# Routing of a mixture-of-experts layer: pair-summed variance, choice of experts in two token halves, block owners on partitions

## The reference

```python
x = layer_norm(DEEPNORM_ALPHA * x + y, ln1_g, ln1_b)
g_logits = x @ w_rg + b_rg                       # 4 groups
grp = argmax(g_logits); p_grp = softmax(g_logits)[grp]
e_logits = (x @ w_re + b_re)[grp]                # 8 experts of that group, 32 in all
top_val, top_idx = top_k(e_logits, 2)
gate = softmax(top_val) * p_grp
# tokens sorted by expert, padded to blocks of rows; every block has one expert
ys = silu(rows @ w_gate[e]) * (rows @ w_up[e]) @ w_down[e], times gate, summed per token
```

## Time and profile before

| | us |
|---|---|
| median of 3 runs | 3631.74 (3631.66 to 3636.03) |
| the profiled execution: its own time | 3633.96 |
| its span, first to last instruction | 3632.7 |
| PE busy in the span | 3414.1 (94%) |
| DVE, ACT, POOL busy | 1570.4, 900.4, 261.7 |

### The profile page before, as it was taken

How to read it: one execution, slowest core, us unless ns; L and a number is a source line. 1 busy time by engine, 2 the same in 40 slices (tenths; PEclk the granted TensorE clock), 3 DMA queues, 4 the chain that set the end, 5 groups by cost and what they waited for, 6 DMA issues and landing times.

```text
span 3632.7 us, 30841 instructions
## 1 busy us (share of the span) xinstructions
PE 3414.1 (94%) x12338; PEld 1862.6 (51%) x12338; DVE 1570.4 (43%) x2766; ACT 900.4 (25%) x1750; POOL 261.7 (7%) x251
## 2 busy tenths in 40 slices
PE   9999998899989899999999999998889997999997
PEld 3468546666654344444444565673447444444443
DVE  6355476466631555444634112324656233211114
ACT  4110453377741100000000111223334031111112
POOL 0012232000000000000000000000000002222221
PEclk9999999999999999999999999999999997999999
DMA  5024212000022111111211101002000108999994
GB/s 229 35 75 167 83 63 90 22 1 1 1 81 93 58 47 47 36 45 36 94 35 41 64 24 41 19 26 82 1 14 11 48 24 340 372 368 369 366 367 164
DMA packets 63243, 370.58 MB, mean 102 GB/s; under 512 B 6826, under 2 KB 13242, under 8 KB 37500
## 3 DMA queue, kind: packets, MB, share of 16 engines
q1 hardware_dynamic: 40492, 187.71, 14.2%
q0 software_dynamic: 22608, 180.89, 13.2%
HBM read 329.16 MB, written 39.41 MB: 101 GB/s over the span
## 4 chain that ended last, share of the span: by engine, by line
PE 83%; DVE 8%; ACT 7%; issue 1%; DMA 1%; SPq 0%; another core or an unknown queue 0%; POOL 0%; DVEq 0%; ACTq 0%; POOLq 0%
PE ps L1298 14%; PE ps L2533 9%; PE ps L1421 7%; PE ps L1596 6%; PE ps L2552 4%; PE ps L837 3%; PE ps L2190 3%; PE ps L1237 3%; PE ps L1598 3%; PE ps L984 2%; PE ps L703 2%; PE ps L840 2%; PE ps L1012 2%; PE ps L646 2%; ACT arena L1064 2%; PE ps L2030 1%
## 5 line engine op out<-in xcount | busy, mean ns | idle before, releaser
L1298 PE MATMUL ps<-arena 128*128 128x512 f32 x1232 | 532.1, 594 | 9.5 <-DVE arena L1324 9.5
L1298 PEld LDWEIGHTS ps<-arena 128*128 128x128 f32 x1232 | 234.3, 190 | 307.0 <-issue 287.1
L2533 PE MATMUL ps<-arena 128*128 128x512 f32 x752 | 331.7, 594 | 0.0
L1421 PE MATMUL ps<-arena 128*128 128x512 f32 x616 | 264.6, 592 | 0.0
L2491 POOL DMA_INDIRECT arena<-in_wgu_dram,arena x47 | 44.1, 939 | 2666.5 <-DVE arena L2450 2414.0
L2533 PEld LDWEIGHTS ps<-arena 128*128 128x128 f32 x752 | 139.8, 191 | 158.1 <-issue 158.1
L1596 PE MATMUL ps<-arena 128*128 128x512 f32 x480 | 209.0, 596 | 0.0
L1421 PEld LDWEIGHTS ps<-arena 128*128 128x128 f32 x616 | 116.6, 189 | 147.9 <-issue 143.8
L1119 DVE TENSOR_SCALAR_CACHE_REDUCE arena<-ps 128x1280 f32<-128x1280 f32 x96 | 139.3, 1488 | 110.1 <-PE ps L984 110.1
L837 PE MATMUL ps<-arena 128*128 128x512 f32 (+1 forms) x432 | 174.7, 558 | 0.0
L2552 PE MATMUL ps<-arena 128*128 128x512 f32 x376 | 169.1, 592 | 0.5 <-DVE arena L2603 0.5
(11 more groups left out here) (375 smaller groups left out, 4943.4 us busy)
## 6 DMA issues: line engine op xcount, KB each, us to landing
arena<-in_wmod_dram SPq DMA_DIRECT2D x24, 1024.0 KB, 5.5
yslot<-arena SPq DMA_DIRECT2D x47, 512.0 KB, 8.7
arena<-in_wup_dram SPq DMA_DIRECT2D x22, 1024.0 KB, 4.8
arena<-in_wout_dram SPq DMA_DIRECT2D x16, 1024.0 KB, 4.8
arena<-in_cf_dram SPq DMA_DIRECT2D x12, 1024.0 KB, 4.8
arena<-in_wdn_dram SPq DMA_DIRECT2D x16, 704.0 KB, 4.0
arena<-in_w2b_dram SPq DMA_DIRECT2D x9, 1024.0 KB, 4.8
arena<-in_ci_dram SPq DMA_DIRECT2D x16, 512.0 KB, 3.5
```

The lines of the kernel that those rows point to most:

```text
L1298: ins = mm(bk(b), left[:, k], right[:, k], k == 0, k == 3)
L1421: ins = mm(bk(b), sb(left + k * 128, 128), right(k), k == 0, k == 10)
L2533: ins = mm(bk(b), sb(XB + i % 2 * 1024 + k * 128, 128), sb(WGU[i % 3] + k * 512, 512), k == 0, k == 7)
```

## The change

- Variance of half 1: ScalarE squares the 8 tiles into 8 buffers, VectorE adds them in pairs, and PE sums the 4 pair sums in bank 7, after the logits of half 0. Half 0 is as before.
- `act_lnscale` raises its event for each tile; the logits wait for each tile.
- `pe_route` has a ring of six banks, and the order: logits 0, pair variance, turning of logits 0, tokens 0 to 3, logits 1, turning of logits 1, tokens 4 to 7, ranks, owners, slots.
- `dve_choose` runs once per half; the gates are formed behind the sums of the choices.
- `dve_place`: block b's owner is found on partition b alone, put on a diagonal and spread over the partitions by a matmul with ones; `widx` comes between the two choices' one-hot work.

```diff
-        for k in range(8):
-            yield from pe_variance(1, k)
+    def pe_pair_variance():
+        yield from claim(7)
+        for k in range(4):
+            P.wait_ge(*(yield ("lnpair", k)))
+            ins = mm(bk(7), con("o1024"), sb(SQ2 + 2 * k * 512, 512), k == 0, k == 3)
+        ins.then_inc(*P.step(("lnv", 1, 7)))
+        held[7] = [("lnx", 1)]
...
+        if tc:
+            A.wait_ge(*(yield ("lnv", 0, 7)))
+        elif k > 3:
+            A.wait_ge(*(yield ("lnv", 0, k - 4)))
...
-        yield from dve_lnscale(1)
+        for k in range(4):
+            V.wait_ge(*(yield ("lnsq", 1, 2 * k + 1)))
+            a, b = (sb(SQ2 + (2 * k + i) * 512, 512) for i in range(2))
+            vt.tensor_tensor(a, a, b, ADD).then_inc(*V.step(("lnpair", k)))
...
+    def pe_logits(tc, banks):
+        n, b = nth["wrt"][0], next(banks)
+        yield from claim(b)
+        P.wait_ge(*wready(n))
+        for k in range(8):
+            P.wait_ge(*(yield ("ln", tc, k)))
+            ins = mm(bk(b, 512, 0, 36), sb(wat(n) + k * 36, 36), sb(XT + k * 1024 + tc * 512, 512), k == 0, k == 7)
...
+        held[b] = [("lt", tc)]
...
+    def pe_turn_logits(tc, banks):
...
+        held[b] = [("lg", tc)]
+
+    def pe_route():
+        banks = ring(range(6))
+        yield from pe_logits(0, banks)
+        yield from pe_pair_variance()
+        yield from pe_turn_logits(0, banks)
+        for j in range(4):
+            yield from pe_tokens(j, banks)
+        yield from pe_logits(1, banks)
+        yield from pe_turn_logits(1, banks)
         for j in range(4, 8):
             yield from pe_tokens(j, banks)
...
+        P.wait_ge(*(yield ("bdiag",)))
+        mm(bk(b, NBLK), con("ones", 0, NBLK), bdiag[0:NBLK], True, True).then_inc(*P.step(("owners",)))
...
     def act_route():
+        for tc in range(2):
+            js = range(4 * tc, 4 * tc + 4)
+            if tc == 0:
+                for j in js[:2]:
+                    yield from act_tokens(j)
+            A.wait_ge(*(yield ("gex", tc)))
+            st.activation(half(ge, tc), half(ge, tc), ACT.Exp).then_inc(*A.step(("gee", tc)))
+            if tc == 0:
+                for j in js[2:]:
+                    yield from act_tokens(j)
+            A.wait_ge(*(yield ("edx", tc)))
+            st.activation(half(ed, tc), half(ed, tc), ACT.Exp).then_inc(*A.step(("ede", tc)))
         for j in range(4, 8):
             yield from act_tokens(j)
...
     def dve_choose():
+        yield from dve_logits(0)
+        yield from dve_lnscale(1)
+        yield from dve_choose_half(0)
+        yield from dve_logits(1)
+        yield from dve_choose_half(1)
...
-        vt.tensor_tensor(cv, incl.rearrange("p (u e) -> p u e", u=1).broadcast_to([128, NBLK, 32]),
-                         con("bidx").rearrange("p (b u) -> p b u", u=1).broadcast_to([128, NBLK, 32]), ALU.is_le).then_inc(*V.step())
...
+        vt.tensor_scalar(owner, incl, con("pidx"), None, ALU.is_le).then_inc(*V.step())
+        vdone()
+        vt.tensor_reduce(bcol, owner, AX.X, ADD).then_inc(*V.step())
+        vdone()
+        vt.tensor_scalar(bcol, bcol, 31.0, 128.0, ALU.min, MUL).then_inc(*V.step())
+        vdone()
+        vt.tensor_scalar(bdiag, con("ident")[:, 0:NBLK], bcol, None, MUL).then_inc(*V.step(("bdiag",)))
         for q, oh in enumerate((oh1, oh2)):
             x, d, du, fb, pm = dest[q]
+            if q:
+                V.wait_ge(*(yield ("owners",)))
+                vt.tensor_scalar(be, bk(bank["owners"], NBLK), con("pidx"), None, ADD).then_inc(*V.step())
+                vdone()
+                vt.tensor_copy(widx.bitcast(U32), be).then_inc(*V.step(("widx",)))
+            vdone()
```

More of the change, by code:

```diff
@@ L2199, in pe_wout2 @@
             yield from pe_mean(tc, 7)
-        for k in range(8):
-            yield from pe_variance(1, k)
+    def pe_pair_variance():
[5 more added lines that the diff above has]
+        held[7] = [("lnx", 1)]
     def act_lnsq(tc, k):
         A.wait_ge(*(yield ("cent", tc, k)))
-        if tc or k > 3:
-            A.wait_ge(*(yield ("lnv", tc - (k < 4), (k - 4) % 8)))
-        st.activation(sb(SQ2 + k % 4 * 512, 512), sb(XT + k * 1024 + tc * 512, 512), ACT.Square).then_inc(*A.step(("lnsq", tc, k)))
+        if tc:
+            A.wait_ge(*(yield ("lnv", 0, 7)))
+        elif k > 3:
+            A.wait_ge(*(yield ("lnv", 0, k - 4)))
+        st.activation(sb(SQ2 + (k if tc else k % 4) * 512, 512), sb(XT + k * 1024 + tc * 512, 512), ACT.Square).then_inc(*A.step(("lnsq", tc, k)))
     def act_lnscale(tc):
@@ L2214, in act_lnscale @@
             A.wait_ge(*(yield ("lnh", tc, k)))
-            st.activation(xx, xx, ACT.Identity, bias=par("l1b", k)).then_inc(*A.step(("ln", tc)))
+            st.activation(xx, xx, ACT.Identity, bias=par("l1b", k)).then_inc(*A.step(("ln", tc, k)))
     def act_wout2():
@@ L2308, in sp_tokens @@
             dma.dma_start(out=x_d[j * 128:(j + 1) * 128, :], in_=sb(XK + j * 1024, 1024)).then_inc(*LD.turn(("xd", j)))
-    def pe_route():
-        banks = ring(range(8))
-        n = nth["wrt"][0]
+    def pe_logits(tc, banks):
+        n, b = nth["wrt"][0], next(banks)
+        yield from claim(b)
         P.wait_ge(*wready(n))
[L2314 to L2325, removed]
+        for k in range(8):
+            P.wait_ge(*(yield ("ln", tc, k)))
+            ins = mm(bk(b, 512, 0, 36), sb(wat(n) + k * 36, 36), sb(XT + k * 1024 + tc * 512, 512), k == 0, k == 7)
+        bank[("logit", tc)] = b
+        ins.then_inc(*P.step(("logit", tc)))
+        held[b] = [("lt", tc)]
+    def pe_turn_logits(tc, banks):
         b = next(banks)
         yield from claim(b)
[L2328 to L2333, removed]
+        P.wait_ge(*(yield ("lt", tc)))
+        for j in range(4):
+            ins = turn(bk(b, 36, off=36 * j), sb(LT + tc * 512 + j * 128, 128, 0, 36), con("ident", 0, 36)[:, 0:36])
+        bank[("lgt", tc)] = b
+        ins.then_inc(*P.step(("lgt", tc)))
+        held[b] = [("lg", tc)]
[4 more added lines that the diff above has]
+        yield from pe_turn_logits(0, banks)
+        for j in range(4):
+            yield from pe_tokens(j, banks)
+        yield from pe_logits(1, banks)
+        yield from pe_turn_logits(1, banks)
         for j in range(4, 8):
@@ L2344, in pe_route @@
         yield from claim(b)
+        P.wait_ge(*(yield ("bdiag",)))
+        mm(bk(b, NBLK), con("ones", 0, NBLK), bdiag[0:NBLK], True, True).then_inc(*P.step(("owners",)))
+        bank["owners"] = b
+        held[b] = [("widx",)]
+        b = next(banks)
+        yield from claim(b)
         for q in range(2):
@@ L2353, in act_route, with half @@
     def act_route():
[L2354 to L2359, removed]
+        for tc in range(2):
[10 more added lines that the diff above has]
+            st.activation(half(ed, tc), half(ed, tc), ACT.Exp).then_inc(*A.step(("ede", tc)))
         for j in range(4, 8):
             yield from act_tokens(j)
+    def half(a, tc):
+        return a[:, 4 * tc:4 * tc + 4]
     def dve_pick(v, ri, n, one, tmp):
@@ L2367, in dve_pick @@
         vdone()
-        vt.tensor_tensor(e, v, m.broadcast_to([128, 8, n]), ALU.is_equal).then_inc(*V.step())
+        vt.tensor_tensor(e, v, m.broadcast_to([128, 4, n]), ALU.is_equal).then_inc(*V.step())
         vdone()
-        vt.tensor_tensor(e, e, wide(ri, n), MUL).then_inc(*V.step())
+        vt.tensor_tensor(e, e, con(ri).rearrange("p (u e) -> p u e", u=1).broadcast_to([128, 4, n]), MUL).then_inc(*V.step())
         vdone()
@@ L2373, in dve_pick @@
         vdone()
-        vt.tensor_tensor(one, e, m2.broadcast_to([128, 8, n]), ALU.is_equal).then_inc(*V.step())
+        vt.tensor_tensor(one, e, m2.broadcast_to([128, 4, n]), ALU.is_equal).then_inc(*V.step())
     def groupwise(a):
-        return a.rearrange("p j (g u) -> p (j g) u", u=1).broadcast_to([128, 32, 8])
+        return a.rearrange("p j (g u) -> p (j g) u", u=1).broadcast_to([128, 16, 8])
     def dve_round(a):
@@ L2384, in dve_round @@
         vdone()
-    def dve_choose():
[L2387 to L2424, removed]
```

52 lines of the change are left out of this document (44 added, 8 removed).

## The result

The changed kernel takes 3626.39 us (median of 11 runs, 3624.44 to 3632.64), the kernel before 3633.6 (11 runs, 3631.66 to 3640.24). The ratio is 0.9979, with a 95% interval of 0.9970 to 0.9987: 0.21% faster, between 0.13% and 0.30%. The profiled execution has a span of 3625.0 us, where it was 3632.7.

A forecast was written before the change was run, and what follows sets the result against it. PE bounds the 47 expert blocks, which follow their start, so the chain of waits in the 77 us before counts. 0.8 + 3.7 + 2.7 - 1.2 = 6.0 us off 3631.74 gives 3625.7; range 3621.0 to 3630.5.

The forecast's parts named there:

- likeliest case: Whole kernel: a change within 0.2% (7.3 us), which a measurement can't tell from none; chance 0.63.
- Variance: Half 1's variance: PE's sums end at 2968.4 instead of 2972.94; root and scaling shift by 4.5 us.
- Logits 1: Half 1's logits: banks hold PE idle 8.4 us, the clock drops, they end at 2991.4 against 2992.23; 0.8 us gained.
- T: The moment logits 1 end, put at 2991.4; 2992.3 if transposes don't count as busy for the clock.
- half-wide steps: Half 1's choice of experts, from logits 1 to the rank matmuls: 13.67 us less 4.8 leaves 8.9.
- Token 7: Its transposes wait for ScalarE's copies of token 4, so ranks start 10.0 us behind logits 1; net 3.7 us gained.
- Place: Block owners and slots: shorter owner steps, widx between the choices; 2.7 us gained (bounds 2.4 to 3.0).
- Gathers: Token gathers land later, behind block 0's weights and the gain tables; 1.2 us lost (ends 0 and 2).
- Logits of 36 columns: Rival: logits 1 don't bring the clock back and take 13.8 us instead of 9.0; 3630.5 us, chance 0.09.
- DMA doesn't bound the experts: Denies the rival that DMA bounds the expert stage and everything follows widx: gain 3.2 us, 3628.5, chance 0.06.
- gathers did not share with the weights behind them: Denies the slower rival: gathers served along with weights of blocks 1 and 2, block 1 turned at 3042; 3641, chance 0.04.
- kept clock: Rival: PE's clock is not lost or returns soon, gathers hardly late; gain 9 us, 3622.5, chance 0.13.

The follow-up runs named there:

- e6: Changed kernel with half 1's 8 squares summed by TensorE one by one, without VectorE's pair sums; ratio to the kernel before 0.9988.
- e1: Changed kernel with logits 1 put before tokens 2 and 3 on TensorE; ratio to the kernel before 0.9973.
- e3: Changed kernel with nine unread 512-column matmuls added in TensorE's idle time before token 2's second transposes; ratio to the kernel before 0.9968.
- e4: Changed kernel with ScalarE's copies of tokens 4 and 5 before the second exponential of half 1; ratio to the kernel before 0.998.
- b1: Kernel before with the block owners' part of the change alone; ratio to the kernel before 0.9991.
- e7: Changed kernel with widx made before the first choice's one-hot work instead of between the two; ratio to the kernel before 0.9978.
- e2: Changed kernel with SyncE's two 0.5 MB gain tables loaded after the second block's output; ratio to the kernel before 0.9981.
- b2: Kernel before with the pair sums of half 1's squares alone, in the variance's old place; ratio to the kernel before 0.9994.

## Why the prediction was right, point by point

The median was put at 3625.7 and came out at 3626.39, while the kernel before, timed beside it, had 3633.6 instead of 3631.74: a gain of 7.2 where 6.0 was forecast, 6.5 of it in the trace. The likeliest case was within 0.2%; measured is 0.21%, with an interval on both sides of that bound.

Term by term, to the first expert matmul, the forecast was 0.8 + 3.7 + 2.7 - 1.2 = 6.0, and the traces give 0.91 + 3.78 + 2.96 - 1.48 = 6.17. The first two terms hold in mechanism and size. That the sum fits so well is partly luck: the last two are off by 0.26 and 0.28 in opposite directions.

- **Variance.** Forecast to end at 2968.4, 10.4 behind the means; 10.62. (Logits 0 were put to 2964.9, where 2958.0 and 7.06 are 2965.06; in the trace their last comes 6.99 behind the means.) That step and the shift of 4.5 us in the scaling (4.3: 2974.74 less 2958.57, against 20.46 before) held. e6 shows the pairs are worth 3.45 of it.
- **Logits 1.** The bank count decided this, and held: PE idle 8.4 us forecast, 8.51 seen, ended by the named bias add; half clock; T gained 0.8 forecast, 0.91 seen. e1 and e3 show both halves of the reason, the queue's order and the clock. Two details were off and cancelled: logits 1 began 0.4 us later than put (the bias add came later, and the 12 transposes took 2.99 us without a pause, not 2.8 with pauses for the copies), and they took 8.54 us instead of 9.0, because the clock returned 2.9 us into them and not 3.9.
- **The half-wide steps.** 13.67 less 4.8 us was to leave 8.9; in e4, where nothing else holds the ranks, they start 8.75 behind logits 1 (42.03 less 33.28).
- **Token 7.** Forecast at T + 10.0, seen at T + 9.90, with ScalarE's copy as the releaser. e4 gives 1.17 back. "By then likely at half clock" was right by little, which is luck: the clock fell just as these transposes began. In e3, where it stayed up, the ranks start 9.14 behind logits 1.
- **Place.** From the ranks' start to the token gather's issue 20.44 before, 17.48 after: 2.96 against 2.7. Some 0.25 of it is the ranks themselves (1.93 instead of 2.18 us to VectorE's first step), because they follow the transposes without a pause and the clock returned under the last of them. Without that, in b1, it is 2.68 (20.44 less 17.76).
- **Gathers.** 1.2 lost forecast, 1.48 measured (8.22 to 9.70). The sign held, and its cause, the shorter lead of the weights, is shown for the first gather by e7. The size is luck in part. Bytes alone, from 3023.0 on, would have both gathers in by 3025.7, as early as the shift alone; the 1.2 us from there to 3026.9 stand on no row. e2 took out a quarter of the bytes for 0.4 us, e7 gave the old lead back and recovered 0.81 of the 1.48, and b2, with the old lead, stands at 9.10 where the kernel before has 8.22. `widx` came 7.22 us behind the ranks' end (7.4 forecast), and the weights were issued 3.78 sooner (3.2 forecast).
- **Rivals.** Logits of 36 columns did bring the clock back (2986 to 2987), so that one falls (the slot matmuls, its argument, did leave the clock at 0.50 here too, 3011 to 3019). DMA doesn't bound the experts: the weights are issued 3.78 us sooner, the last gather 6.48. The gathers did not share with the weights behind them to the point of a loss: the second took 6.59 us, and block 1 was turned at 3027.22, not near 3042. A kept clock would have been worth 3.17 us (e3); the rival's 9 us against 6.0 said 3. (Its 3622.5 should be 3622.7.)
- The Trainium skill (TensorE: Matmul & The Clock Gate, section on the transpose mode) says that a transpose doesn't count as PE-busy in the same way. The forecast kept to the rows instead. That was right here. In e1 the clock returned at 2997.1 with nothing but transposes on PE since 2993.22, and in the changed kernel it returned in 3003 to 3004, 3.4 us after PE resumed with transposes alone in the first 2.0. T, at 2991.88 on the trace's clock and 2991.3 less the drift of 0.56, lies by 2991.4 and not by 2992.3, but that fit alone would decide little, with the two details above in it.

What was not seen beforehand is how much the new order costs, since the forecast never set the parts against each other: it called the wait of logits 1 a gain of 0.8, where pairs alone give 3.1.

## What to carry to other kernels

Moving work into an idle stretch of a queue written by hand moves what stands behind it too: count the banks, name who frees each and where that instruction stands in its own engine's order, before calling a finer wait a gain. A stall of some microseconds on TensorE costs again as lower speed behind it; here keeping it busy through the stall was worth 3.2 us (e3), about as much as the squares that the pair sums save (3.45 at the variance, e6). And when a result that starts transfers (`widx`) is moved behind other work, the lead of those transfers over the next ones is a term of the sum.

## What the runs showed of the hardware

- The granted clock was 0.50 after TensorE had been idle for 8.51 us in the changed kernel, 4.84 us in e1 and 5.66 us in b2. It returned some 6 us after work resumed in the changed kernel, 5 in b2 (whose variance so ended 0.4 us ahead of the forecast), 3.2 in e1, and 3.4 us after token 7's transposes began. With the clock at 0.50 for the first 2.9 us of them, logits 1 took 8.54 us instead of 7.06.
- Float32 transposes alone (4 of the logits, then 24 of 128x128) brought the clock back in e1.
- The first gather of tokens took 4.24 to 4.34 us from issue to use with 3.1 MB of weights issued 12 us ahead (three kernels), and 5.44 to 6.46 us with them 8 us ahead (nine kernels).
- VectorE steps of 256, 128 and 16 elements took 0.42, 0.29 and 0.17 us: halving the width from 256 saved 0.13 us, just under a third.
